# The input loaded from two queues, and the first modulation chunk placed inside the first norm

## What is computed

```
cond = silu(c)
mod  = cond @ mod_w[0] + mod_b[0]            # six vectors of 1024
sh1, sc1, g1, sh2, sc2, g2 = split(mod, 6)
h = x * rsqrt(mean(x*x) + eps) * norm_mix_g[0]
h = h * (1 + sc1) + sh1
y = dsa_attention(h, ...)                    # projections of h, index scores, top 64 keys, attention
```

## Time and profile before

| | us |
|---|---|
| median of 3 runs | 740.59 (739.83 to 742.02) |
| profiled execution, its own time | 741.73 |
| its span, first to last instruction | 739.9 |
| TensorE matmul busy | 704.2 (95%) |
| VectorE busy | 532.5 (72%) |
| ScalarE busy | 414.3 (56%) |
| GpSimd busy | 128.4 (17%) |
| HBM traffic over the span | 211 GB/s |
| mean granted TensorE clock | 0.993 |

### The profile page before, as it was taken

How to read it: one execution, slowest core, us unless ns; L and a number is a source line. 1 busy time by engine, 2 the same in 40 slices (tenths; PEclk the granted TensorE clock), 3 DMA queues, 4 the chain that set the end, 5 groups by cost and what they waited for, 6 DMA issues and landing times.

```text
span 739.9 us, 17363 instructions
## 1 busy us (share of the span) xinstructions
PE 704.2 (95%) x6920; PEld 642.7 (87%) x6920; DVE 532.5 (72%) x897; ACT 414.3 (56%) x681; POOL 128.4 (17%) x113
## 2 busy tenths in 40 slices
PE   3899999899999999999999999999999999999996
PEld 1578989569798999999998888889799999999994
DVE  4866778585678878778867876866487667666765
ACT  5355745565464656576567754354566555555553
POOL 1000101001035443444304175410000000000000
PEclk9899999999999999999999999999999999999999
DMA  8989978955756666555575045249435555555521
GB/s 308 396 320 401 363 264 284 330 211 217 286 180 208 247 228 229 176 170 182 185 279 175 31 165 181 89 140 395 150 114 177 185 185 193 171 175 191 174 83 58
DMA packets 46216, 157.14 MB, mean 212 GB/s; under 512 B 6048, under 2 KB 7344, under 8 KB 46160
## 3 DMA queue, kind: packets, MB, share of 16 engines
q1 hardware_dynamic: 41040, 139.87, 54.2%
q0 software_dynamic: 2960, 10.10, 3.9%
q10 hardware_dynamic: 2160, 6.38, 2.2%
HBM read 155.28 MB, written 1.05 MB: 211 GB/s over the span
## 4 chain that ended last, share of the span: by engine, by line
PE 87%; DVE 5%; issue 3%; ACT 2%; POOL 1%; DMA 1%; ACTq 0%; DVEq 0%; POOLq 0%
PE up L418 13%; PE up L420 13%; PE up L419 13%; PE acc L418 10%; PE acc L419 9%; PE acc L420 9%; PE gv L463 4%; PE acc L621 3%; DVE wlo L1234 2%; PE misc L522 1%; PE up L817 1%; PE up L804 1%; DMA ident<-in_ident 1%; PE acc L792 1%; DVE tmp L1264 1%
## 5 line engine op out<-in xcount | busy, mean ns | idle before, releaser
L1234 DVE TENSOR_TENSOR wlo<-raw,whi 128x1024 fp32r<-128x1024 f32 x188 | 252.2, 1356 | 56.9 <-ACT whi L873 52.2
L418 PE MATMUL up<-hh,whi 128*128 128x256 f32 x832 | 237.4, 285 | 2.3 <-DVE hl L1269 1.9
L420 PE MATMUL up<-hh,wlo 128*128 128x256 f32 x832 | 235.3, 283 | 0.0
L419 PE MATMUL up<-hl,whi 128*128 128x256 f32 x832 | 235.3, 283 | 0.0
L873 ACT ACTIVATE whi<-raw 128x1024 fp32r<-128x1024 f32 x185 | 192.5, 1052 | 43.8 <-PE acc L420 21.5
L418 PEld LDWEIGHTS up<-hh,whi 128*128 128x128 f32 x832 | 159.5, 192 | 8.9 <-issue 5.0
L419 PEld LDWEIGHTS up<-hl,whi 128*128 128x128 f32 x832 | 159.6, 192 | 0.0
L420 PEld LDWEIGHTS up<-hh,wlo 128*128 128x128 f32 x832 | 159.5, 192 | 0.0
L1552 DVE SCALAR_TENSOR_TENSOR ffn<-up,conv,ffn 128x254 f32<-128x254 f32 (+1 forms) x176 | 72.6, 474 | 44.4 <-ACT ffn L1081 44.0
L418 PE MATMUL acc<-ah,whi 128*128 128x256 f32 x352 | 99.8, 284 | 0.6 <-DVE wlo L1234 0.6
L419 PE MATMUL acc<-al,whi 128*128 128x256 f32 x352 | 99.6, 283 | 0.0
(11 more groups left out here) (266 smaller groups left out, 946.4 us busy)
## 6 DMA issues: line engine op xcount, KB each, us to landing
raw<-in_w SPq DMA_DIRECT2D x188, 512.0 KB, 3.7
mraw<-in_mw SPq DMA_DIRECT2D x32, 512.0 KB, 6.6
arena<-in_mw SPq DMA_DIRECT2D x32, 512.0 KB, 7.9
arena<-in_mw POOLq DMA_DIRECT2D x16, 512.0 KB, 4.6
raw<-in_w SPq DMA_DIRECT2D x12, 256.0 KB, 13.0
tmp<-in_mw ACTq DMA_DIRECT2D x4, 512.0 KB, 6.4
ffn<-in_mw ACTq DMA_DIRECT2D x4, 512.0 KB, 8.9
mraw<-in_mw ACTq DMA_DIRECT2D x4, 512.0 KB, 16.4
```

The costliest lines, as they stand in the source:

```text
L418: pe.matmul(out, w_h, xh, start=first, stop=False, skip_group_check=skip)
L419: pe.matmul(out, w_h, xl, start=False, stop=False, skip_group_check=skip)
L420: return pe.matmul(out, w_l, xh, start=False, stop=last, skip_group_check=skip)
L1234: dve.tensor_tensor(wlo[:, n % SPL, :], raw[:, n % RAW, :], whi[:, n % SPL, :].bitcast(F32), ALU.subtract).then_inc(lo_ready, 1)
```

## The change

Half of x is issued by ScalarE, ahead of its three small DMAs, and SyncE issues only the other half. On TensorE `gemv(0)` runs behind the sums and ahead of their transposition, through the hook `first` of `norm`, so the order is now: sums, `gemv(0)`, transposition of the sums, `spread_root`, `gemv(1)`. The wait for `cond` moves ahead of the sums. Nothing else changes on any engine.

```
-            for k in range(0, KT, 2):
+            for k in range(0, KT // 2, 2):
                 sp_.dma_start(x[:, k:k + 2, :], t["x"][:, k:k + 2, :]).then_inc(x_in, 16)
             load_m(0)
             load_early(1)
...
             pe.wait_ge(set_up, 5)
             pe.wait_ge(ones_in, 16 * N_ONES)
-            norm(0, 0, None)
             pe.wait_ge(cond_ready, 1)
-            gemv(0)
+            norm(0, 0, None, first=lambda: gemv(0))
             spread_root(0, misc[:, T:2 * T])
             gemv(1)
             columns(0)
...
+            for k in range(KT // 2, KT, 2):
+                act.dma_start(x[:, k:k + 2, :], t["x"][:, k:k + 2, :]).then_inc(x_in, 16)
             act.dma_start(craw[:], t["cond"]).then_inc(cond_in, 16)
             for dst, name in ((prm[:, 0:PRM_IN, :], "prm"), (jrow[:], "jrow")):
                 act.dma_start(dst, t[name]).then_inc(prm_in, 16)
```

## The result

The changed kernel takes 744.43 us (median of 6 executions, 743.33 to 745.88) beside 740.55 for the kernel before (6 executions, 739.83 to 742.9). The ratio is 1.0047, with a 95% interval of 1.0025 to 1.007: slower by about 3.9 us or half a per cent. I had forecast 742.5 with a range of 739.6 to 744.6. The profiled execution of the changed kernel took 745.88 for a span of 744.0.

A forecast was written before the change was run, and what follows sets the result against it. TensorE is busy 95% of the span, so the start of its dense matmul stream counts. Reciprocal later by 2.1 (order) + 1.4 (`jrow`) = 3.5 us, less 1.64 idle: +1.9 on 740.59 gives 742.5, range 739.6 to 744.6.

The forecast's parts named there:

- the sums were late: At the start on TensorE: late `jrow` delays ScalarE's squares by 1.7 us, leaving the sums 1.4 us later.
- The order's term: `gemv(0)` ahead of the sums' transposition: VectorE's reciprocal 2.1 us later, the first split 0.4 to 0.5 us later.
- The absorbed 1.64 us: VectorE's idle time between the angle table's end and the first split, 1.64 us, absorbs that much of the reciprocal's slip.
- two more places at the mean of the two, 1.47 us, put `jrow` at 10.2: ScalarE's queue: two DMAs of x ahead move `jrow`'s landing from 7.28 to 10.2, at 1.47 us per place.
- The upper bound of 13.6: Latest `jrow` landing: ScalarE's half of x lands at 9.2, then three small DMAs follow at 1.47 us each.
- the rival of a very late `jrow`: `jrow` on ScalarE's queue lands at 12 to 13.6: +3.4 to +5 us, 744 to 745.6; chance 0.16.
- The last sum had 0.3 us to spare: On TensorE, the last sum started at about 12.2 against squares ended at 11.85, so 0.3 us of lateness costs nothing.
- `ident`'s shift: Landing of the constant `ident` on GpSimd's queue, 10.95 before: shift priced at zero, half a us to either side.
- TensorE's path against VectorE's: Before the first projections: TensorE's `columns(0)` ends at 24.9, VectorE wants it at 25.2, so VectorE stays later.
- The rival by the clock: TensorE's gapless sums and `gemv(0)` bring the higher clock early, saving 2.5 us: 738.6 at best; chance 0.10.
- The rest moves rigidly: Behind about 28 us, the dense matmul stream moves rigidly with the moment at which it begins.

## Why the prediction was right, and where not

**Direction and range: right. The size: half.** +1.9 was forecast and +3.9 measured. The range held it by 0.2 us, and with luck: the sums were late by 3.87 us where 1.4 were forecast, 2.5 more, and the order cost 1.05 where 2.1 were forecast, 1.0 less. Without the second error the split would have been another 1 us later.

**The order's term** was 2.1 us at the reciprocal and 0.4 to 0.5 at the split; alone it gave 2.1 and 0.53. In the changed kernel it was only 1.05: the reciprocal's slip of 4.95 less the sums' 3.9. There `gemv(0)` took 2.8 us and the transposition 0.6, for 3.4 and 1.0. The clock came up in the middle of `gemv(0)`, at about 18 us: its matmuls that start by 16.8 take 1.06 us each, those from 17.95 on 0.59. In the kernel before all sixteen take 1.01 to 1.06. The absorbed 1.64 us is exact: 4.95 - 1.64 = 3.31, and the split is 3.34 later.

**The term that was mis-sized is "two more places at the mean of the two, 1.47 us, put `jrow` at 10.2".** It landed at 12.54. The price per place was good (`craw` 9.35, `prm` 11.11, `jrow` 12.54: 1.8 and 1.4 apart). What I missed is that the third place itself moved, from 7.3 to 9.4. With two DMAs of 4 KB ahead it stayed at 7.1, so this part has to do with x: with half of x gone from SyncE's queue the 512 KB quarters start earlier beside ScalarE's DMAs (the first is issued at 1.7 and not at 2.6), and two DMAs of x are ahead. Which of the two it is was not separated. The upper bound of 13.6 held it, and the rival of a very late `jrow` (12 to 13.6, +3.4 to +5) is what happened; I gave it 0.16. Its own sum takes the 0.3 us twice: by the working for 10.2 it is +3.6 to +5.2.

**"The last sum had 0.3 us to spare" was wrong.** The squares end 3.88 us later and the last sum starts 3.87 us later. What was taken for room is the time from the last square's end to the start of the last sum, 0.44 us in both kernels. This was 0.3 of the miss.

**`ident`'s shift** was priced at nothing within half a us; it came 1.3 us earlier, which the prediction itself had named as a sign of being wrong. It cost the forecast nothing, since the squares set the sums.

**TensorE's path against VectorE's**: VectorE the later one, as forecast. TensorE was ready to go on much earlier (its bank's copy at 22.83 against 21.48, 1.35 later only).

**The rival by the clock** did not come for the better: the record shows 0.50 from 24.7 to 35.0, against 23.6 to 30.4 before. Of the 4.1 us by which the profiled span is longer, 3.34 are at the split, 0.5 came by the end of this stretch, and 0.8 by 60 us, behind the second low stretch; 0.55 came back between 440 and 500 us, where the profiled execution of the kernel before was late. "The rest moves rigidly" held from 60 to 430 us, with a lag of 4.6 throughout, and not around the low stretches. That the second stretch comes from the change is not shown. For it speaks that all six executions of the changed kernel have a mean clock of 0.987 to 0.991, where 49 of 79 of the kernel before have more.

## What to carry to other kernels

Before you give a queue a larger load, look at what small things stand behind it and who waits for them: here 80 KB of small constants (`prm` and `jrow`) for a layer that starts hundreds of us later gated the first norm. On a queue that runs beside a dense stream, count DMAs and not bytes, and put the small ones on the stream's own queue, ahead of it. When a result is moved to be ready "just in time", check every engine whose queue it heads, not only the engine that consumes it. And where a change is worth 1 us at the start, compare executions by their mean clock, for the place in a trace and the median can point in different directions.

## What the runs showed of the hardware that I had not expected

- A DMA of 4 KB ahead on a queue costs those behind it nearly as much as one of 256 KB. Beside SyncE's stream `craw`, `prm` and `jrow` landed 2.0 and 2.3 us apart (7.1, 9.1, 11.4), without it 0.3 to 0.4 us apart (6.6, 6.9, 7.4).
- x in halves on two queues landed 3.4 us earlier for the same bytes (5.8 for 9.2), and SyncE's stream behind it 1.5 us earlier (13.4 for 14.9), 1.1 of that by its earlier issue.
- Starting TensorE's dense part earlier by 1.35 us gave nothing in the median: the low stretch of the clock ended at 29.3 in place of 30.4, and second and third ones of 3.4 us came at 43.0 and at 432.1.
